# Second norm of a hybrid decoder from token columns, with five weight pieces split and lowered ahead of it

## The reference

```python
for i in range(DEPTH):
    h = rms_norm(x, norm_w[i]) * (1.0 + scale) + shift
    hc = rms_norm(ctx, norm_w[i]) * (1.0 + c_scale) + c_shift
    ...
    x = x + gate * o
return rms_norm(x, final_norm_w)

def rms_norm(x, w):
    y = xf * lax.rsqrt(jnp.mean(xf * xf, axis=-1, keepdims=True) + EPS)
```

## Time and profile before

| | us |
|---|---|
| median of 3 runs | 2425.8 (2420.58 to 2426.4) |
| the profiled execution | 2424.95 |
| its span | 2423.1 |
| PE busy | 2336.0 (96%) |
| PE weight loads | 1941.8 (80%) |
| DVE, ACT, POOL busy | 1097.6, 1128.7, 1162.7 |
| last product of layer 0 ends | 882.2 |
| first product of layer 1 starts | 899.51 |

### The profile page before, as it was taken

The page is one execution under the profiler, slowest core; times in us unless marked ns, Lnnn a source line. Parts: engine busy times, 40 slices in busy tenths (PEclk is TensorE's granted clock), DMA queues, the critical chain, the costliest instruction groups (busy, mean ns, idle before and its releaser), DMA issues.

```text
span 2423.1 us, 59202 instructions
## 1 busy us (share of the span) xinstructions
PE 2336.0 (96%) x25854; PEld 1941.8 (80%) x25854; DVE 1097.6 (45%) x2337; ACT 1128.7 (47%) x2042; POOL 1162.7 (48%) x634
## 2 busy tenths in 40 slices
PE   6999999999999978999999999999999999999997
PEld 2576777777778856788888888888888888888997
DVE  3143344333340037555555655555555555553223
ACT  3343333333342237654565456644664466544443
POOL 2232333333335545456644765466546664563544
PEclk9999999999999989999999999999999999999998
DMA  9855555555543221233323332333223322336553
GB/s 375 322 210 208 196 209 215 189 184 189 205 188 125 87 96 49 104 109 105 109 84 106 106 114 72 107 106 114 93 94 105 115 98 82 114 106 235 191 183 115
DMA packets 99347, 352.15 MB, mean 145 GB/s; under 512 B 10768, under 2 KB 15248, under 8 KB 96784
## 3 DMA queue, kind: packets, MB, share of 16 engines
q1 hardware_dynamic: 99088, 348.36, 40.8%
HBM read 336.13 MB, written 12.19 MB: 144 GB/s over the span
## 4 chain that ended last, share of the span: by engine, by line
PE 90%; DVE 4%; DMA 2%; ACT 2%; issue 1%; POOL 1%; SPq 0%; DVEq 0%; ACTq 0%
PE bank L884 9%; PE bank L886 8%; PE bank L885 8%; PE bank L695 8%; PE bank L697 8%; PE bank L696 8%; PE bank L981 4%; PE bank L652 3%; PE bank L1124 2%; PE bank L924 2%; PE bank L925 2%; PE bank L926 2%; PE bank L1126 2%; PE bank L1125 2%; PE bank L1093 2%; PE bank L1078 2%
## 5 line engine op out<-in xcount | busy, mean ns | idle before, releaser
L479 POOL TENSOR_TENSOR wl<-raw,wh 128x1024 fp32r<-128x1024 f32 x215 | 517.2, 2413 | 615.3 <-ACT wh L474 615.3
L884 PE MATMUL bank<-hh,wh 128*128 128x512 f32 (+1 forms) x1040 | 409.8, 394 | 19.5 <-DVE hl L1834 14.4
L407 POOL TENSOR_TENSOR wl<-raw,wh 128x1024 fp32r<-128x1024 f32 x85 | 207.3, 2448 | 405.3 <-ACT wh L402 405.1
L886 PE MATMUL bank<-hh,wl 128*128 128x512 f32 (+1 forms) x1040 | 381.5, 367 | 1.6 <-issue 1.5
L885 PE MATMUL bank<-hl,wh 128*128 128x512 f32 (+1 forms) x1040 | 380.8, 366 | 0.0
L474 ACT ACTIVATE wh<-raw 128x1024 fp32r<-128x1024 f32 x232 | 245.6, 1061 | 277.4 <-PE bank L926 121.4
L695 PE MATMUL bank<-hh,wh 128*128 128x512 f32 x864 | 345.7, 400 | 5.9 <-ACT scratch L1511 3.3
L697 PE MATMUL bank<-hh,wl 128*128 128x512 f32 x864 | 337.6, 391 | 0.0
L696 PE MATMUL bank<-hl,wh 128*128 128x512 f32 x864 | 337.3, 390 | 0.0
L884 PEld LDWEIGHTS bank<-hh,wh 128*128 128x128 f32 x1040 | 197.5, 190 | 60.3 <-issue 15.1
L886 PEld LDWEIGHTS bank<-hh,wl 128*128 128x128 f32 x1040 | 197.3, 190 | 35.7 <-issue 1.9
(11 more groups left out here) (299 smaller groups left out, 4531.1 us busy)
## 6 DMA issues: line engine op xcount, KB each, us to landing
raw<-w_in SPq DMA_DIRECT2D x259, 512.0 KB, 3.6
raw<-w_ada SPq DMA_DIRECT2D x101, 512.0 KB, 5.4
raw<-w_out SPq DMA_DIRECT2D x84, 512.0 KB, 3.6
scratch<-w_ada SPq DMA_DIRECT2D x59, 512.0 KB, 5.9
scratch<-keep_g SPq DMA_DIRECT2D x15, 1024.0 KB, 5.7
scratch<-w_in SPq DMA_DIRECT2D x23, 512.0 KB, 6.9
raw<-w_gate SPq DMA_DIRECT2D x22, 512.0 KB, 5.2
scratch<-xT SPq DMA_DIRECT2D x2, 4096.0 KB, 12.9
```

The lines of the kernel that those rows point to most:

```text
L407: eng.tensor_tensor(fl[h % SPLIT], ring[ring_slot("half", h)], fh[h % SPLIT].bitcast(F32), ALU.subtract)\
L479: eng.tensor_tensor(buffers(s)[1], raw[:, s % RAW, :], buffers(s)[0].bitcast(F32), ALU.subtract)\
L884: pe.matmul(ps, w[:, k * P:(k + 1) * P], hhv[:, kk, t0:t1], start=first and k == k0, stop=False)
L886: done = pe.matmul(ps, r[:, k * P:(k + 1) * P], hhv[:, kk, t0:t1], start=False, stop=last and k == k1 - 1)
```

## The change

1. Pieces 0 to 4 are loaded as soon as layer 0's last piece is lowered, copied by ACT after the square of tile 14 and lowered by POOL in the order 0, 3, 2, 4, 1. Pieces 3 and 4 have four new buffers `w_more`, which lie where `front_room` was; pieces 1 and 2 change their buffers of `wh` and `wl`, since the last three pieces of layer 0 leave them one after the other. A small Sqrt stands ahead of the copies.
2. The last square is not added by POOL. PE sums over features with tokens in the partitions: four products of 128 x 2 from `n_acc` and four from the last square. ACT takes the root of 128 x 8, DVE its reciprocal, and multiplies it by the unit matrix to `n_eye` (128 x 512). PE multiplies `n_eye` by ones into bank 7, which is the row of reciprocals in all partitions; DVE's scales read it from there.
3. The copy of tile 0 stands right behind its affines.
4. PE takes pieces 2 and 3 together, then two quarters of q, the turns, and two more.
5. The Exp of `a_log` stands behind the first Exp of beta; the affine coefficients of layer 1 are made ahead of the output tiles.

The diff, without the counts of `n_added`, `n_summed` and `n_root` that follow from it (`ADDED` is 14):

```diff
-            return [cut(HALF * P) for _ in range(RING - RAW)], cut(KT * SILW), [cut(T), cut(T)]
+            return [cut(HALF * P) for _ in range(RING - RAW)], cut(HALF * P)[:, 0:KT * SILW], [cut(T), cut(T)]
...
         n_rinv = cut(T)
-        n_full = [cut(T), cut(T)]
-        n_t = [cut(T), cut(T)]
-        n_odd = n_t[0]
+        n_col = cut(2 * NT)
+        n_eye = cut(T)
+        n_odd = cut(T)
...
         scope.close()
+        cut(KT * T)
+        w_more = [cut(HALF * P, F32R) for _ in range(4)]
+
+        scope.close()
         cut(CTAT)
...
+        SPLITS = [0, 3, 2, 4, 1]
         NDELTA = 2 + 12 * KH
...
             o = s - NDELTA
+            if s in (3, 4):
+                return w_more[2 * (s - 3)], w_more[2 * (s - 3) + 1]
+            if s in (1, 2):
+                return wh[:, 3 - s, :], wl[:, 3 - s, :]
             if o >= 0 and o % 5 < 2:
...
             else:
-                eng.wait_ge(sem("rear_lo"), s + 1 if o < 0 else NDELTA + 8 + o // 2 + 1)
+                n = SPLITS.index(s) if s < len(SPLITS) else s
+                eng.wait_ge(sem("rear_lo"), n + 1 if o < 0 else NDELTA + 8 + o // 2 + 1)
...
             o = s - NDELTA
-            if o >= 2:
+            if s < SPLIT:
+                eng.wait_ge(sem("front_done"), NHALF0 - (2, 0, 1)[s])
+            elif s == 4:
+                eng.wait_ge(sem("ada_summed"), NEARLY + 1)
+                eng.wait_ge(sem("unit_done"), UNITS)
+            elif s == 5:
+                eng.wait_ge(sem("rear_done"), 2)
+            elif o >= 2:
                 eng.wait_ge(sem("rear_done"), s - 4)
...
                 eng.wait_ge(sem("w6_made"), KH - 1)
-            elif s >= SPLIT:
+            elif s > 5:
                 eng.wait_ge(sem("rear_done"), s - SPLIT + 1)
...
-            eng.wait_ge(sem("rear_hi"), s + 1)
+            eng.wait_ge(sem("rear_hi"), (SPLITS.index(s) if s < len(SPLITS) else s) + 1)
             eng.tensor_tensor(buffers(s)[1], raw[:, s % RAW, :], buffers(s)[0].bitcast(F32), ALU.subtract)\
...
             sp.wait_ge(sem("front_lo"), NHALF0)
-            for s in range(2):
+            for s in range(5):
                 rear_load(sp, s, w_in1[s, :, :])
...
             sp.dma_start(keep_x1, xv[:, :, SEG:T]).then_inc(sem("x1_kept"), 16)
-            for s in range(2, 12):
+            for s in range(5, 12):
                 rear_load(sp, s, w_in1[s, :, :])
...
-            def square_sum():
-                pe.wait_ge(sem("n_added"), KT - 1)
-                pe.matmul(pb[6][:, :], ones[:, :], n_acc, start=True, stop=True).then_inc(sem("n_summed"), 1)
+            def square_columns():
+                pe.wait_ge(sem("n_added"), ADDED)
+                for c in range(NT):
+                    pe.matmul(pb[6][:, 2 * c:2 * c + 2], n_acc[:, c * P:(c + 1) * P], ones[:, 0:2], start=(c == 0), stop=False)
+                pe.wait_ge(sem("n_squared"), 2 * KT)
+                for c in range(NT):
+                    done = pe.matmul(pb[6][:, 2 * c:2 * c + 2], n_sq[1][:, c * P:(c + 1) * P], ones[:, 0:2],
+                                     start=False, stop=(c == NT - 1))
+                done.then_inc(sem("n_summed"), 1)
+                pe.wait_ge(sem("n_root"), 3)
+                pe.matmul(pb[7][:, :], ones[:, :], n_eye, start=True, stop=True).then_inc(sem("n_summed"), 1)
...
                     late_sum()
-            square_sum()
+            square_columns()
...
             wait_lo(pe, 2)
-            products(2, 0, HALF, PA[:, :], 0, T, False, True, "h_lo", 1)
             wait_lo(pe, 3)
-            products(3, 0, 1, pb[4][:, :], 0, T, False, False, None, 1)
+            for k in range(HALF):
+                products(2, k, k + 1, PA[:, :], 0, T, False, k == HALF - 1, "h_lo", 1)
+                products(3, k, k + 1, pb[4][:, :], 0, T, False, k == HALF - 1, None, 1)
+            q_quarter(0, 0, pb[5])
+            q_quarter(0, 1, pb[5])
             pe.wait_ge(sem("ba_copied"), 1)
...
             done.then_inc(sem("ba_turned"), 1)
-            products(3, 1, HALF, pb[4][:, :], 0, T, False, True, None, 1)
-            for q in range(4):
+            for q in range(2, 4):
                 q_quarter(0, q, pb[5])
...
                 act.wait_ge(sem("n_summed"), layer + 1)
-                act.activation(n_rinv, pb[6][:, :], ACT.Sqrt, scale=1.0 / D, bias=eps[:, 0:1])\
-                   .then_inc(sem("n_root"), 1)
+                dst, src = (n_col, pb[6][:, 0:2 * NT]) if layer else (n_rinv, pb[6][:, :])
+                act.activation(dst, src, ACT.Sqrt, scale=1.0 / D, bias=eps[:, 0:1]).then_inc(sem("n_root"), 1)
...
                 made = norm_affine(layer, first)
+                if layer and first == 0:
+                    norm_hi(layer, first, made)
+                    first += 1
+                    made = norm_affine(layer, first)
                 for k in range(first + 1, end):
...
                     square(t - 1)
+            act.activation(n_col[:, 0:2], eps[:, 0:2], ACT.Sqrt)
+            for s in SPLITS:
+                rear_split_hi(act, s)
             act.wait_ge(sem("x1_ready"), 2 * KT)
...
             act.wait_ge(sem("aff_ready"), 5)
-            for s in range(3):
-                rear_split_hi(act, s)
             norm_group(1, 0, KT // 2)
...
-            rear_split_hi(act, 3)
             act.wait_ge(sem("rear_done"), 3)
             act.activation(b_fm, PA[:, :], ACT.Copy).then_inc(sem("ba_copied"), 1)
-            act.activation(b_t[5][:, 0:2 * VH], smc("a_log"), ACT.Exp)
-            rear_split_hi(act, 4)
             rear_split_hi(act, 5)
...
             ch.link(act.activation(b_t[2], b_t[1], ACT.Exp, scale=-1.0))
+            act.activation(b_t[5][:, 0:2 * VH], smc("a_log"), ACT.Exp)
             act.activation(b_t[3], b_t[2], ACT.Ln, bias=1.0).then_inc(sem("soft_ready"), 1)
...
                 dve.wait_ge(sem("n_root"), layer + 1)
-                ch.link(dve.reciprocal(n_rinv, n_rinv))
+                if layer == 0:
+                    ch.link(dve.reciprocal(n_rinv, n_rinv))
+                    return
+                ch.link(dve.reciprocal(n_col, n_col))
+                by = n_col.rearrange("p (c o) -> p c o", o=2)[:, :, 0:1].to_broadcast([P, NT, P])
+                eye = ident.rearrange("p (c n) -> p c n", c=1).to_broadcast([P, NT, P])
+                dve.tensor_tensor(n_eye.rearrange("p (c n) -> p c n", n=P), eye, by, ALU.mult).then_inc(sem("n_root"), 1)
+                dve.wait_ge(sem("n_summed"), 3)
...
                     dve.wait_ge(sem("h_hi"), layer * KT + k - 8 + 1)
-                dve.tensor_tensor(norm_t(layer, k), xv[:, k, :], n_rinv, ALU.mult).then_inc(sem("n_scaled"), 1)
+                dve.tensor_tensor(norm_t(layer, k), xv[:, k, :], pb[7][:, :] if layer else n_rinv, ALU.mult)\
+                   .then_inc(sem("n_scaled"), 1)
...
             dve.wait_ge(sem("x_in"), 16 * (GROUPS // 2 + 2))
+            affine(1, 0, KT, NEARLY + 1)
             for t in range(KT):
...
                                              op0=ALU.mult, op1=ALU.add).then_inc(sem("x1_ready"), 1)
-            affine(1, 0, KT, NEARLY + 1)
             dve.wait_ge(sem("x1_ready"), 2 * KT)
...
                     add_squares(k)
-            for k in range(KT - 3, KT):
+            for k in range(KT - 3, KT - 1):
                 add_squares(k)
...
-            for s in range(3):
+            for s in SPLITS:
                 rear_split_lo(pool, s)
...
-            for s in range(3, 8):
+            for s in range(5, 8):
                 rear_split_lo(pool, s)
...
```

More of the change, by code:

```diff
@@ L42 @@
 MODBLK = 12
+ADDED = KT - 2
 SILW = 62
@@ L635, in _ @@
                     p = (1, 2, 4).index(j)
-                    sp.wait_ge(sem("n_added"), 2 * (KT - 1) + 2 * p + 2)
+                    sp.wait_ge(sem("n_added"), ADDED + KT - 1 + 2 * p + 2)
                     store(5 + p)
@@ L1333, in _ @@
                 out_half(n)
-            pe.wait_ge(sem("n_added"), 2 * (KT - 1))
+            pe.wait_ge(sem("n_added"), ADDED + KT - 1)
             pe.matmul(pb[4][:, 0:SEG], ones[:, :], f_acc, start=True, stop=True).then_inc(sem("n_summed"), 1)
@@ L1788, in _ @@
                 if t >= 3:
-                    act.wait_ge(sem("n_added"), KT - 1 + t - 2)
+                    act.wait_ge(sem("n_added"), ADDED + t - 2)
                 act.activation(f_sq[t % 2] if t else f_acc, x1[:, t, :], ACT.Square).then_inc(sem("n_squared"), 1)
                 act.activation(f_out[:, t, :], x1[:, t, :], ACT.Copy, scale=smc("final_w")[:, t:t + 1])
-            act.wait_ge(sem("n_summed"), 3)
+            act.wait_ge(sem("n_summed"), 4)
             act.activation(f_rinv, pb[4][:, 0:SEG], ACT.Sqrt, scale=1.0 / D, bias=eps[:, 0:1])\
@@ L2361, in _ @@
                     rear_split_lo(dve, NDELTA + (4 * t + 7 if t else 11))
-            dve.wait_ge(sem("n_root"), 3)
+            dve.wait_ge(sem("n_root"), 4)
             dve.reciprocal(f_rinv, f_rinv).then_inc(sem("n_scaled"), 1)
@@ L2463, in add_final @@
                 if k >= 2:
```

(2 more changed lines are left out.)

## The result

| | before | after |
|---|---|---|
| median, us | 2425.89 (2420.58 to 2431.1, 12 runs) | **2433.53** (2425.37 to 2440.14, 12 runs) |
| ratio | | **1.0029**, 95% interval 1.0015 to 1.0042 |
| the profiled execution | 2424.95, span 2423.1 | 2426.99, span 2425.2 |

The change makes the kernel slower by 0.3%, where I forecast 2421.2. The profiled execution is one of its faster ones, 2.04 us over the profiled one of before.

What follows compares the result with a forecast made beforehand. PE was busy 96%; the second norm left PE, then ACT's affines and beta set the pace. Norm, PE and beta terms summed to -4.65 us at 939.15, forecasting 2421.2 us (chance 0.51), range 2415.5 to 2426.5.

Steps and rivals of the forecast that it cites:

- what is gained before 939.15 goes through to the end: From DVE's copy of the small sums (939.15 us before) into the head loop: the 4.65 us gained there carries through.
- the three rivals: Whole kernel: more than the sum, -7.7 us (chance 0.24); gain hidden, -1.5 us (0.2); slower, +5.1 us (0.05).
- the one on the slow side: ACT's last square waits behind piece 4's copy, its load landing at 891.2: +5.1 us, 2430.9; chance 0.05.
- Last square: ACT, second norm: queued behind the early copies, it ends at 884.3 instead of 883.76, +0.5 us.
- Column sums, root, reciprocal: Second norm on PE, ACT, DVE: sums save 1.05 us, root 0.45 (to 0.28), reciprocal 3.15 (to 0.18 plus a link).
- Diagonal product: DVE, second norm: 0.68 us alone, held by POOL until 887.5 and ending at 888.05, so +2.1 us.
- Ones product: PE, second norm: the new product at half clock after idle time, +2.1 us.
- First product: PE, odd block: starts 2.5 us after affine 0, at 893.4, where it started at 899.51 before.
- g ready: Beta and decay on DVE and ACT: 7.3 us after the turns, at 928.5, 5.85 us earlier than before.
- PE's idle time ahead of the sums: Beta and decay: PE ends its four q quarters at 924.1 and waits 4.4 us for g.
- The sums: PE's 16 small fp32 sums at half clock: 5.9 us by a factor of 1.6 from weight loads, ending at 934.45.
- The copy: DVE's copy of the small sums: starts at 934.5 instead of 939.15, -4.65 us in all.

Runs made afterwards that it cites:

- shift 0 to 32: Shift: PE instructions by which the loop's 256-instruction block ends differ from the kernel before, mod 256. Without the change 2425.9 to 2435.2 us; with it 2423.5 to 2433.5, 2437.5, 2433.6.
- shift 0: Block ends as in the kernel before: that kernel itself 2425.9 us; changed kernel with 56 small idle-time products (224 PE instructions) 2423.5 us, ratio 0.9989.
- the new norm alone: Kernel before with only the norm by token columns, plus 56 small products to keep block ends in place: 2423.84 us, ratio 0.9991.
- shift 32: Block ends moved 32 instructions: changed kernel as made 2433.5 and 2437.5 us, with 64 small products 2433.6; kernel before with 8 small products 2435.2.
- 128: Block ends moved 128 instructions: changed kernel with 24 small products 2447.06 us, ratio 1.0087; kernel before with 32 small products 2451.14 us, ratio 1.011.
- 192: Block ends moved 192 instructions: changed kernel with 40 small products in PE's idle time, 2427.99 us, ratio 1.0009 to the kernel before.
- the run with 56 products: Changed kernel with 56 small unused products (224 PE instructions) in PE's idle time of the norm: 2423.48 us, ratio 0.9989 to the kernel before.

## Why the prediction was wrong

The step that failed is the sentence "so what is gained before 939.15 goes through to the end". I took the rest of the program for a thing of fixed length behind a start that moves. It isn't: what it costs depends on how many instructions PE's list has ahead of it. Its 32 more cost 9 to 14 us (shift 0 to 32, in either column), against a gain of 2.7 at shift 0. No term of my sum and no rival had that, though the diff shows 8 products of two columns and a new one where one stood. None of the three rivals came about either; in the one on the slow side, the load of piece 4 landed by 878.85 and held ACT for 1.27 us, which cost the last square 0.2.

Point by point, each from the last x1, in the profiled execution:

- **Last square.** Forecast +0.5 from the copies queued ahead of it; measured +0.2 (it starts at 880.76). The load of piece 4 landed 1.7 us ahead of the last x1, as forecast (881.5 against 883.1).
- **Column sums, root, reciprocal.** 1.05, 0.27 and 0.20 us at L701, L1385 and L1859, as taken from the like forms.
- **Diagonal product.** Forecast 2.1 with the hold by POOL. Measured 1.17 in this execution, and 2.16 to 2.63 in the nine others with the whole change; with POOL idle (the new norm alone) it took 0.69. The mechanism was right: in all ten DVE ended 0.54 to 0.56 us behind a POOL instruction. That in this one it met the end of the instruction before was luck, and saved 0.9.
- **Ones product** 2.08 (forecast 2.1, half clock); scales from the bank 0.68 (forecast 0.7).
- **First product** 9.3 us after the last x1 (forecast 10.3); turns end 37.7 after (38.1); g ready 44.8 after (45.4).
- **PE's idle time ahead of the sums** 3.93 (4.4). **The sums** 7.0 us, at 0.43 each: 1.9 times the full-clock time, not the 1.6 times that I had from weight loads. This is the mis-sized term, 1.1 us. I had weighed the Trainium skill's page "TensorE: Matmul & The Clock Gate", section "LDWEIGHTS (loading the stationary operand)", whose formula for a load, columns divided by 1.2 in ns, has no term for the clock. The trace disagrees, and more than I had believed: a load of these sums took 192 ns at 2.4 GHz (before) and 333 at 1.2 (after).
- **The copy**, 51.9 after, forecast 51.4.

So the sum of parts was off by half a microsecond in 4.65, and the forecast by 12. That the sum came so close is in part luck: the first product was 1.0 us earlier than forecast and the sums 1.1 longer, and in the two other profiles at shift 32 the copy came 53.19 us after the last x1, 1.8 later than forecast.

What stays open: why the waits of one shift come only in some heads (the first four at 32, from the third on at 128, the last three at 192), although the place in the code is the same. The traces do show a drift: counted in PE's instructions, the packet of one place in the loop starts some 7 earlier in each head (from 347 to 250 over 13 heads in the run with 56 products), so that a burst meets it differently from head to head. Which heads then wait isn't worked out. And that PE stands because the next packet isn't there yet is inferred from the place and the time of the waits; no run changed the length of a packet's transfer by itself.

## What to carry to other kernels

A loop written out in full has a length in instructions, and where the blocks of the instruction queue end in it is a property of everything ahead of it. Look for PE waits "<- issue" inside bursts of small products; if they repeat from turn to turn, add idle-time instructions in steps of 16 or 32 and see whether the time moves. Judge an edit ahead of such a loop only with the count of its instructions kept, mod 256, or over several shifts: here the shift was worth up to 30 us and the edit some 3 to 6.

## What I had not expected of the hardware

- By count and size, PE's instructions come in packets of 16 KB, 256 instructions. All 79 waits of over 0.4 us without a releaser in the loop, over all 16 profiles, stood at instruction 192 or 193 of a block, 0.4 to 2 us long, and ended 2.1 to 2.8 us after a packet began. In each of them at least 74 of the 96 products just before were small ones of 32 rows, of which 128 with their loads take 1.5 us; no such wait stood in a stretch of wide products alone (0.23 us each).
- 8 such products of 32 x 32 in a stretch where PE had stood idle for 12 us made the kernel before 9 us slower; 60 made it 3 to 4 us faster.
- A small float32 product (128 x 32, two matmuls with their loads) takes 0.427 us at 1.2 GHz and 0.225 at 2.4.
